# Attention heads in pairs: alternating score and value matmuls, four score banks and one transpose bank

## What is computed

```
for i in range(S // Q_BLOCK):
    q0, q1 = i * Q_BLOCK, (i + 1) * Q_BLOCK
    s = jnp.einsum('bhqd,bhkd->bhqk', q[:, :, q0:q1], k[:, :, :q1]) * scale
    s = s + cum[:, :, q0:q1, None] - cum[:, :, None, :q1]
    causal = (q0 + jnp.arange(Q_BLOCK))[:, None] >= jnp.arange(q1)[None, :]
    p = jax.nn.softmax(jnp.where(causal, s, neg), axis=-1)
    outs.append(jnp.einsum('bhqk,bhkd->bhqd', p.astype(v.dtype), v[:, :, :q1]))
```

## Time and profile before

| what | value |
|---|---|
| runs | 756.77, 758.88, 760.61 us; median 758.88 |
| profiled execution | 758.44 us |
| its span, first to last instruction | 756.6 us |
| mean granted TensorE clock | 0.966 of full |
| TensorE busy | 683.3 us, 90% |
| VectorE busy | 307.8 us, 41% |
| ScalarE busy | 167.9 us, 22% |
| loop over the heads | about 127.9 to 214.9 us of the span |

### The profile page before, as it was taken

How to read it: one execution, slowest core, us unless ns; L and a number is a source line. 1 busy time by engine, 2 the same in 40 slices (tenths; PEclk the granted TensorE clock), 3 DMA queues, 4 the chain that set the end, 5 groups by cost and what they waited for, 6 DMA issues and landing times.

```text
span 756.6 us, 10005 instructions
## 1 busy us (share of the span) xinstructions
PE 683.3 (90%) x3369; PEld 385.7 (51%) x3369; DVE 307.8 (41%) x700; ACT 167.9 (22%) x291; POOL 28.5 (4%) x49
## 2 busy tenths in 40 slices
PE   2799999899999999798999979989999998899894
PEld 0478856677788467464344333433433343343342
DVE  2247987665724256652322221231222222212214
ACT  2010142111341113022222211221222122122221
POOL 7001111000000000000000000000000000000000
PEclk9789999999999999899999989999999999999997
DMA  8998989323331000484699999999999999999951
GB/s 307 387 378 288 389 310 344 120 109 112 112 139 56 0 1 3 162 339 167 247 427 428 424 424 430 422 426 429 428 423 427 426 429 424 424 430 427 423 234 56
DMA packets 43133, 225.66 MB, mean 298 GB/s; under 512 B 3488, under 2 KB 3520, under 8 KB 29414
## 3 DMA queue, kind: packets, MB, share of 16 engines
q1 hardware_dynamic: 41528, 224.43, 73.6%
q10 hardware_dynamic: 1582, 0.94, 0.5%
HBM read 224.31 MB, written 1.05 MB: 298 GB/s over the span
## 4 chain that ended last, share of the span: by engine, by line
PE 58%; DMA 30%; DVE 5%; SPq 2%; issue 2%; ACT 1%; ACTq 1%; DVEq 0%
DMA raw<-n_w_experts_gate_up_dram 27%; PE bank L1119 13%; PE bank L1415 13%; PE bank L1364 4%; PE bank L1399 4%; PE bank L1239 4%; PE bank L1271 4%; DMA ring<-in_w_ada_dram 3%; PE bank L1405 2%; PE bank L1147 2%; PE bank L1423 1%; PE bank L1375 1%; DVE work L748 1%; SPq L323 1%; SPq L319 1%
## 5 line engine op out<-in xcount | busy, mean ns | idle before, releaser
L1119 PE MATMUL bank<-work,ring 128*128 128x256 f32 x512 | 118.0, 388 | 1.4 <-ACT work L482 1.4
L1415 PE MATMUL bank<-raw,hT 128*32 128x512 f32 x832 | 99.8, 635 | 18.4 <-DMA raw<-n_w_experts_gate_up_dram 18.4
L1119 PEld LDWEIGHTS bank<-work,ring 128*128 128x128 f32 x512 | 98.4, 195 | 17.1 <-issue 2.6
L1399 PE MATMUL bank<-raw,hT 128*128 128x512 f32 x224 | 99.9, 599 | 2.8 <-ACT hT L593 2.8
L1019 DVE TENSOR_TENSOR sg<-sg,bank 128x256 f32<-128x256 f32 x27 | 11.4, 421 | 170.2 <-ACT sg L602 170.2
L1415 PEld LDWEIGHTS bank<-raw,hT 128*32 128x32 f32 x832 | 31.5, 116 | 85.4 <-issue 85.4
L1375 PE MATMUL bank<-y,ST 128*128 128x512 f32 x224 | 70.7, 438 | 2.3 <-DVE y L1028 2.3
L1399 PEld LDWEIGHTS bank<-raw,hT 128*128 128x128 f32 x224 | 41.4, 190 | 61.0 <-issue 58.5
L1405 PE MATMUL bank<-raw,aT 128*128 128x512 f32 x112 | 51.7, 604 | 7.4 <-ACT aT L607 7.4
L611 ACT ACTIVATE y<-bank,wcol 128x512 fp32r<-128x512 f32 x54 | 34.2, 684 | 108.5 <-PE bank L1405 54.3
L602 ACT ACTIVATE sg<-bank 128x256 f32<-128x256 f32 x27 | 17.2, 636 | 182.2 <-PE bank L1415 100.7
(11 more groups left out here) (289 smaller groups left out, 612.3 us busy)
## 6 DMA issues: line engine op xcount, KB each, us to landing
raw<-n_w_experts_gate_up_dram SPq DMA_DIRECT2D x53, 2048.0 KB, 16.7
raw<-in_w_experts_down_dram SPq DMA_DIRECT2D x53, 1024.0 KB, 18.4
ring<-in_w_ada_dram SPq DMA_DIRECT2D x12, 2048.0 KB, 18.4
ring<-in_w_in_dram SPq DMA_DIRECT2D x9, 2048.0 KB, 13.1
ring<-in_w_out_dram SPq DMA_DIRECT2D x2, 2048.0 KB, 7.8
ring<-in_w_attn_out_dram SPq DMA_DIRECT2D x1, 2048.0 KB, 18.9
ring<-in_w_conv_out_dram SPq DMA_DIRECT2D x1, 2048.0 KB, 7.9
ring<-in_w_shared_gate_up_dram SPq DMA_DIRECT2D x1, 2048.0 KB, 7.8
```

What stands on the lines that cost most here:

```text
L1119: ins = mm(b[:, kk * SEQ:(kk + 1) * SEQ], w[:, k, m * PART:(m + 1) * PART], h1T[:, k, :], start=(k == 0), stop=(k == KD - 1))
L1399: ins = mm(psU[:, :], hT[:, k, :], wg[:, k, :], start=(k == 0), stop=(k == KD - 1))
L1415: ins = mm(psU[c:c + 32, :], hT[:, k, c:c + 32], w_gu(s)[:, k, :], start=(k == 0), stop=(k == KD - 1))
```

## The change

Heads are treated in pairs p = 0 to 3 of an even and an odd head.

- `S_B` becomes four banks, 0, 1, 3 and 5, head h using entry h modulo 4. `PT_B` becomes the single bank 2.
- `scores(p)` issues the matmuls of both heads in alternation: q by k of the even head, of the odd head, the forget term of both, the mask of both, first for 128 keys and then for 256. Its waits: `ada2_out` 8 ahead of pair 1 (bank 5 was in use before), the exponentials of the pair two before from pair 2 on. Ahead of pair 0, `ada2_out` 7 is waited for.
- `transposes(h)` waits, from head 1 on, until head h - 1 was copied out.
- `values(p)` issues the six matmuls of a pair in alternation, behind the copies of both heads, and signals `o_done` by 2 at the end.
- The loop's order for a pair is: scores of the next pair, gate half, transposes of the even head, gate half, transposes of the odd head, gate half, values of the pair, gate half. In the last pair the means stand behind the third gate half, and the values behind them.

The programs of VectorE and ScalarE keep their order; they use other banks.

```diff
-        S_B, PT_B, O_B, M_B = [0, 1], [2, 3], 4, [6, 7]
+        S_B, PT_B, O_B, M_B = [0, 1, 3, 5], 2, 4, [6, 7]
...
-            def scores(h):
-                b, base, j = bank[S_B[h % 2]], 64 * (h % 2), h // 2
-                if h >= 2:
-                    pe.wait_ge(exp_done, h - 1)
+            def scores(p):
+                heads = (2 * p, 2 * p + 1)
+                if p == 1:
+                    pe.wait_ge(ada2_out, 8)
+                if p >= 2:
+                    pe.wait_ge(exp_done, 2 * p - 2)
                 for q, o, keys in ((0, 0, PART), (1, PART, SEQ)):
                     qs = slice(q * PART, (q + 1) * PART)
-                    mm(b[:, o:o + keys], qk[base:base + HD, j, qs], qk[base:base + HD, KC + j, 0:keys], start=True, stop=False)
...
+                    for h in heads:
+                        base = 64 * (h % 2)
+                        mm(bank[S_B[h % 4]][:, o:o + keys], qk[base:base + HD, p, qs], qk[base:base + HD, KC + p, 0:keys],
+                           start=True, stop=False)
...
             def transposes(h):
                 pe.wait_ge(p_ready, h + 1)
-                if h >= 2:
-                    pe.wait_ge(pT_out, h - 1)
+                if h >= 1:
+                    pe.wait_ge(pT_out, h)
...
+            def values(p):
+                b = bank[O_B]
+                pe.wait_ge(pT_out, 2 * p + 2)
+                if p >= 1:
+                    pe.wait_ge(o_out, p)
+                for c, pc, t, first in ((0, 0, 0, True), (PART, PART, 0, True), (PART, SEQ, 1, False)):
+                    for h in (2 * p, 2 * p + 1):
+                        base = 64 * (h % 2)
+                        ins = mm(b[base:base + HD, c:c + PART], v_sb[:, t, h * HD:(h + 1) * HD], probT[:, h % 2, pc:pc + PART],
+                                 start=first, stop=(c == 0 or not first))
+                ins.then_inc(o_done, 2)
...
+            for p in range(HEADS // 2):
+                if p + 1 < HEADS // 2:
+                    scores(p + 1)
+                gate_half(4 * p + 1)
+                transposes(2 * p)
+                gate_half(4 * p + 2)
+                transposes(2 * p + 1)
+                gate_half(4 * p + 3)
+                if p + 1 < HEADS // 2:
+                    values(p)
+                    gate_half(4 * p + 4)
```

More of the change, by code:

```diff
@@ L536, in _ @@
                     a.wait_ge(pT_done, h - 1)
-                ps = bank[S_B[h % 2]]
+                ps = bank[S_B[h % 4]]
                 a.activation(prob[:, h % 2, 0:PART], ps[:, 0:PART], ACT.Exp, bias=st2[:, 6:7] if h % 2 == 0 else st2[:, 10:11],
@@ L802, in head_pT @@
                     v.wait_ge(o_done, h - 1)
-                v.tensor_copy(probT[:, h % 2, :], bank[PT_B[h % 2]][:, 0:3 * PART]).then_inc(pT_out, 1)
+                v.tensor_copy(probT[:, h % 2, :], bank[PT_B][:, 0:3 * PART]).then_inc(pT_out, 1)
             def head_out(h):
@@ L1180, in scores @@
                     qs = slice(q * PART, (q + 1) * PART)
-                    mm(b[:, o:o + keys], qk[base:base + HD, j, qs], qk[base:base + HD, KC + j, 0:keys], start=True, stop=False)
-                    mm(b[:, o:o + keys], AU[base:base + 40, j, qs], BU[base:base + 40, j, 0:keys], start=False, stop=False)
-                    ins = mm(b[:, o + keys - PART:o + keys], ident_b[:, :], causal[:, :], start=False, stop=True)
-                ins.then_inc(s_done, 1)
+                    for h in heads:
+                        base = 64 * (h % 2)
+                        mm(bank[S_B[h % 4]][:, o:o + keys], qk[base:base + HD, p, qs], qk[base:base + HD, KC + p, 0:keys],
+                           start=True, stop=False)
@@ new lines, in scores @@
+                    for h in heads:
+                        base = 64 * (h % 2)
+                        mm(bank[S_B[h % 4]][:, o:o + keys], AU[base:base + 40, p, qs], BU[base:base + 40, p, 0:keys],
+                           start=False, stop=False)
+                    for h in heads:
+                        ins = mm(bank[S_B[h % 4]][:, o + keys - PART:o + keys], ident_b[:, :], causal[:, :], start=False, stop=True)
+                        if q == 1:
+                            ins.then_inc(s_done, 1)
@@ L1186, in transposes @@
             def transposes(h):
                 pe.wait_ge(p_ready, h + 1)
-                if h >= 2:
-                    pe.wait_ge(pT_out, h - 1)
+                if h >= 1:
+                    pe.wait_ge(pT_out, h)
                 for i in range(3):
                     o = i * PART
-                    ins = tr(bank[PT_B[h % 2]][:, o:o + PART], prob[:, h % 2, o:o + PART], ident[:, :])
+                    ins = tr(bank[PT_B][:, o:o + PART], prob[:, h % 2, o:o + PART], ident[:, :])
                 ins.then_inc(pT_done, 1)
[L1195 to L1199, removed]
-                b = bank[O_B]
[L1201 to L1204, removed]
@@ L1210, in _, with gate_half @@
             pe.wait_ge(ada2_out, 6)
+            pe.wait_ge(ada2_out, 7)
             scores(0)
[L1212 to L1224, removed]
+            def gate_half(i):
+                u = 10 + i // 2
+                if i % 2 == 0:
+                    arrived(UNIT_PIECE[u])
+                    if u >= 12:
+                        pe.wait_ge(unit_out_act, 8 + u - 11)
+                project_in(u, (i % 2,))
+            for p in range(HEADS // 2):
[9 more added lines that the diff above has]
+                    gate_half(4 * p + 4)
                 else:
@@ L1232, in _ @@
                         ins.then_inc(mean_done, 1)
-                values(h)
+                    values(p)
             def project(w, src, i, done):
```

## The result

| | before | changed |
|---|---|---|
| median | 758.88 us (755.39 to 761.36, 7 runs) | 765.11 us (763.02 to 767.43, 7 runs) |
| profiled execution | 758.44 us, span 756.6 | 764.81 us, span 763.0 |
| mean granted clock | 0.966 | 0.963 |

The changed kernel is slower: ratio 1.0088, 95% interval 1.0062 to 1.0113. The forecast was 763.3 us, in a range from 757.5 to 767.0.

The account below looks back on a forecast made before the run. TensorE sets the pace before; afterwards VectorE's work between paired transposes makes it wait. 758.44 less 1.06 gained plus 5.5 for clock falls gives 762.9, with 0.44 for the median 763.3 us; range 757.5 to 767.0.

Parts of the forecast that it names:

- falls on the path: Clock falls behind waits at odd heads: 1.9 us each for two waits of 3.8, 1.7 for that of 3.3.
- Part 1 and 2: TensorE scores and values: fewer shape changes gain 0.65 us a pair; full overlap takes scores to 2.09, values to 1.00.
- Part 3: Between paired heads' transposes VectorE needs 7.03 to 7.57 us, TensorE has 3.77; it waits 1.7, 3.8, 3.8 and 3.3.
- The clock: After long TensorE waits the granted clock falls to its 1.2 GHz level, slowing gate halves; charged 5.5 us in all.
- The median: Whole kernel: 762.9 us for the profiled execution plus 0.44 for the median gives 763.3, 0.6% slower.
- the second (rows don't overlap): Row groups in the scores don't overlap: 767.2 us, half an overlap 765.2; chance 0.20 for both.
- the third: VectorE's stretches between paired transposes are much shorter, 1.5 us each, with no fall: 752 to 755 us; faster, chance 0.10.
- the first: Clock holds at the new waits: 757.8 us, one fall 759.6, two 761.5; chance of holding mostly 0.20.

Follow-up runs that it names:

- `e_fill`: Changed kernel with TensorE repeating the gate half just made, ahead of the transposes of heads 1, 3, 5 and 7; 759.92 us.
- `e_best`: Changed kernel with two pairs' scores and one gate half before head 0's transposes, later transposes spread out, VectorE's taps redistributed; 740.49 us.
- `e_serial`: Changed kernel with each head's score matmuls in one piece, even head then odd head, instead of alternating; 777.47 us.
- `e_taps`: Changed kernel with two rounds of VectorE taps moved from before the odd head's normalization to behind the odd head's copy; 747.04 us.
- `e_spread`: Changed kernel with only TensorE's loop order altered, putting more work between transposes and two gate halves before head 0's; 743.43 us.
- `e_spread_serial`: Changed kernel's matmuls in the spread-out TensorE order, but each head's scores and values in one piece instead of alternating; 756.88 us.

## Why the prediction was right, step by step

| step, by the changed kernel's first profile | predicted | measured |
|---|---|---|
| scores of a pair | 2.09 | 2.05 |
| transposes 0 to 1, 2 to 3, 4 to 5, 6 to 7 | 7.15, 7.57, 7.57, 7.03 | 7.14, 7.41, 7.40, 6.88 |
| waits at heads 1, 3, 5, 7 | 1.7, 3.8, 3.8, 3.3 | 3.13, 3.46, 3.46, 2.93 |
| heads 1 to 2 and 3 to 4, without the fall | 13.87 each | 13.96 each |
| head 5 to 6 (no fall there) | 11.78 | 11.75 |
| head 7 to the projection, without the fall | 6.86 | 7.15 |
| head 0's transposes to the projection, without falls | 75.70 | 75.65 (75.65 in the second profile) |
| falls on the path | 5.5 | 6.01 (4.84) |

The measured 75.65 is 81.66 (138.22 to 219.88) less the falls: 1.68 at head 1, 2.64 at head 3, 1.69 at head 7. Each is the excess over what transposes behind a wait and their gate half take at full clock: 3.94 us to the values (192.41 to 196.35), and 3.84 at head 7, where the means follow (0.39 for the transposes, 3.45 for the gate half as in `e_fill`, 210.21 to 213.66). The second profile gives 80.49 less 1.47, 1.68 and 1.69.

That the sum without falls is met to 0.05 us is in part luck. The four stretches that VectorE sets were 0.49 us too long in the prediction, and those at TensorE's pace 0.44 too short, most of it in the last: from the values to the projection it took off 0.32, and that stretch lasts 1.49 (218.39 to 219.88) as it lasted 1.47 before. The 12 us of saved TensorE time are in no sum of the prediction; its own terms give four times 2.05 + 0.60, 10.6, and `e_best`, busy for 72.32 us where the kernel before is for 84.83 with one fall of 1.7 in it, shows 10.8.

- **Part 1 and 2, cheaper matmuls:** right. Row groups do run side by side: the nearest row, four column groups, was a good guide. Only the gain of the values was mis-sized: alternation gives them 0.27 us, not the 0.65 between 1.30 and 0.65. How much of the 1.96 us that a pair of scores gained (4.01 in `e_serial`, 2.05 here) is overlap and how much fewer changes of shape was not separated by a run; the two rows of 0.54 above speak for full overlap, 1.28 of it.
- **Part 3, the distance between the transposes:** right, and shown from both sides, by taking work out of the stretch (`e_taps`) and by lengthening it (`e_spread`). The first stretch was met to 0.01, the others were charged 0.15 to 0.17 too much. In that of heads 2 to 3 the output copy was charged at its 0.42 but handed on after 0.34 (165.16 to 165.50), and transposes without a wait ahead of them reach their copy in 0.53, not 0.59 (161.00 to 161.53). The waits of heads 3, 5 and 7 came out 0.3 to 0.4 shorter than predicted: about half is the shorter stretch, and the rest is that the profile puts the end of the gate half's row (161.33 + 3.62 = 164.95) 0.18 later than the 3.77 of the prediction does. The wait at head 1 was put at 1.7, on the assumption that the clock falls behind head 0 as it did before. It did in one of two profiles. In the other the fall came behind head 1 instead, on the path. So the number of falls on the path came out as forecast, three in both profiles, but in the first by luck: at heads 1, 3 and 7 and not 3, 5 and 7.
- **The clock:** right as a price (`e_fill`), at 1.9 and 1.7 a fall for 1.5 to 2.6. That each of the three long waits would be followed by one was too simple: one of 3.46 was not. Over the four traces with such waits at odd heads, 2.9 to 3.5 us long, 12 of 14 were followed by a fall.
- **The median:** 6.2 us slower against 4.4 forecast. In the first profile 4.90 of 6.37 us lie in the loop (the wait sum and the falls), 1.1 at the very end, where the clock fell during the last eight scatter matmuls (3.68 against 2.59 us), and the rest ahead of that. The second pair of profiles differs by 2.8. Outside the loop, one and the same program moves as much: head 0's transposes of the changed kernel come at 138.22 and 136.04 us in its two profiles, and from the projection to the end of the span it is 543.1 and 544.5 us. Whether the part outside the loop is more than chance stays open.
- **Rivals:** the second (rows don't overlap) fell with the 2.05 us of a pair; the third with stretches right to 0.17; the first is what `e_fill` made true, 759.9 where 757.8 was forecast for no fall at all, and 1.84 of the difference is its filler ahead of head 1. The way out was order and not a faster VectorE, as `e_spread` shows, where VectorE's program is untouched. The Trainium skill (TensorEngine Tiling (Array Packing), PSUM Bottleneck) says that packing speeds up TensorE but not the reading out of PSUM. The trace agrees in so far as TensorE now waits 12.98 us for VectorE at the odd heads. But what filled VectorE there was mostly taps, which read no PSUM: in `e_taps`, with every copy out of PSUM in place, the waits were at most 0.30.

## What to carry to other kernels

When two engines hand work back and forth, what counts is the time between two hand-overs, not the busy shares: before regrouping work on the faster-made engine, add up what the other must do between any two of them and keep at least as much other work there. A wait of 3 us is dearer than 3 us, because the clock may fall behind it; and a cheap check on a regrouping is to try the same matmuls in a second order, since here the order was worth some 21 us, and the alternation 12 to 13, the falls of the clock that came without it included.

## What the runs showed of the hardware that I had not expected

- The clock can fall with no idle time at all: 4.8 us after the first of the scores made head by head (127.13), at 131.9 us in `e_serial`, for 10 us (granted clock 0.50 from 132 to 142, TensorE busy all the time). Alternating between the two row groups, four heads of scores (127.83 to 132.03 in the changed kernel) kept it at full, 1.00.
- Twelve value instructions of two column groups of 64, one group after the other, took 1.15 us (1.14 to 1.15 in four places of `e_spread_serial`) where 12 x 0.108 is 1.30: the two groups overlap in part without any alternation.
- Waits of equal length (3.46 us) in the same program were followed by a fall in three of four cases over two profiles, and a fall cost 1.47 to 2.64 us.
